# Overflow buffers of a mixture-of-experts stage in two sets, and the last pair's rows brought to their tokens by a matrix product

## The reference, cut to what matters

```
def hierarchical_moe(h, w_rg, b_rg, w_re, b_re, w_gate, w_up, w_down):
    ...
    weights = (g_w * e_w).astype(h.dtype)
    expert = (g_idx * EXPERTS_PER_GROUP + e_idx).reshape(-1)
    ...
    hg = lax.ragged_dot(xs, w_gate, sizes)
    hu = lax.ragged_dot(xs, w_up, sizes)
    ys = lax.ragged_dot(jax.nn.silu(hg) * hu, w_down, sizes)
    ys = ys[inv].reshape(N, TOP_K, D)
    out = jnp.einsum('nkd,nk->nd', ys, weights)
```

## Time and profile before

| | us |
|---|---|
| median of three runs | 1244.88 |
| the profiled execution | 1245.46 |
| its span, first to last instruction | 1243.7 |
| PE busy in it | 1151.6 (93%) |
| DVE, ACT, POOL busy | 663.8, 524.6, 102.8 |
| weights and everything else moved | 252.67 MB, mean 203 GB/s |

### The profile page before, as it was taken

How to read it: one execution, slowest core, us unless ns; L and a number is a source line. 1 busy time by engine, 2 the same in 40 slices (tenths; PEclk the granted TensorE clock), 3 DMA queues, 4 the chain that set the end, 5 groups by cost and what they waited for, 6 DMA issues and landing times.

```text
span 1243.7 us, 20589 instructions
## 1 busy us (share of the span) xinstructions
PE 1151.6 (93%) x8444; PEld 972.2 (78%) x8444; DVE 663.8 (53%) x1217; ACT 524.6 (42%) x916; POOL 102.8 (8%) x165
## 2 busy tenths in 40 slices
PE   6999999999999999989999999899987899889893
PEld 4888788999999888888999998878876654545451
DVE  4555567888745455467898745676445411111113
ACT  5444445555533434544665643464532211111112
POOL 5000000000000000000040000000100022111110
PEclk9999989999999999989999999899996999999897
DMA  9444446777455343336876556333263599999962
GB/s 291 139 153 152 144 138 189 215 230 203 155 185 169 119 170 129 125 119 188 233 207 177 180 171 186 102 102 103 69 245 128 203 420 419 416 418 386 361 279 110
DMA packets 199512, 252.67 MB, mean 203 GB/s; under 512 B 19807, under 2 KB 179083, under 8 KB 187131
## 3 DMA queue, kind: packets, MB, share of 16 engines
q1 hardware_dynamic: 185312, 223.55, 52.9%
q0 software_dynamic: 13744, 27.67, 6.4%
q10 hardware_dynamic: 363, 0.14, 0.0%
HBM read 273.34 MB, written 11.53 MB: 229 GB/s over the span
## 4 chain that ended last, share of the span: by engine, by line
PE 75%; DVE 7%; DMA 6%; ACT 5%; issue 3%; POOL 1%; DVEq 0%; ACTq 0%; POOLq 0%; SPq 0%
PE ps L775 17%; PE ps L776 16%; PE ps L777 16%; PE ps L2512 7%; PE ps L2525 3%; DMA wo<-in_w_exp_gate,wrow 3%; DMA wo<-in_w_exp_down,wrow 2%; ACT whi L747 2%; PE ps L717 2%; PE ps L2115 2%; DVE wlo L756 1%; PE ps L2116 1%; PE ps L2182 1%; PE ps L2504 1%; DMA wo<-in_w_exp_up,wrow 1%
## 5 line engine op out<-in xcount | busy, mean ns | idle before, releaser
L775 PE MATMUL ps<-xhi,whi 128*128 128x272 f32 (+2 forms) x1424 | 428.9, 301 | 20.4 <-DVE xlo L771 10.9
L776 PE MATMUL ps<-xlo,whi 128*128 128x272 f32 (+2 forms) x1424 | 412.6, 290 | 0.0
L777 PE MATMUL ps<-xhi,wlo 128*128 128x272 f32 (+2 forms) x1424 | 411.5, 289 | 0.0
L756 DVE TENSOR_TENSOR wlo<-raw,whi 128x2048 fp32r<-128x2048 f32 (+1 forms) x115 | 259.6, 2257 | 158.6 <-ACT whi L747 158.5
L775 PEld LDWEIGHTS ps<-xhi,whi 128*128 128x128 f32 x1424 | 274.3, 193 | 35.0 <-issue 25.2
L747 ACT ACTIVATE whi<-raw 128x2048 fp32r<-128x2048 f32 (+1 forms) x115 | 216.2, 1881 | 149.8 <-PE ps L777 149.7
L776 PEld LDWEIGHTS ps<-xlo,whi 128*128 128x128 f32 x1424 | 274.0, 192 | 0.9 <-issue 0.5
L777 PEld LDWEIGHTS ps<-xhi,wlo 128*128 128x128 f32 x1424 | 273.3, 192 | 0.0
L775 PE MATMUL ps<-hhi,whi 128*128 128x272 f32 (+1 forms) x352 | 100.7, 286 | 0.7 <-DVE wlo L756 0.6
L776 PE MATMUL ps<-hlo,whi 128*128 128x272 f32 (+1 forms) x352 | 100.2, 285 | 0.0
L777 PE MATMUL ps<-hhi,wlo 128*128 128x272 f32 (+1 forms) x352 | 99.9, 284 | 0.0
(11 more groups left out here) (420 smaller groups left out, 1589.6 us busy)
## 6 DMA issues: line engine op xcount, KB each, us to landing
raw<-in_w_up SPq DMA_DIRECT2D x88, 512.0 KB
raw<-in_w_in SPq DMA_DIRECT2D x33, 1024.0 KB
ada<-in_w_ada POOLq DMA_DIRECT2D x48, 512.0 KB, 5.1
raw<-in_w_exp_gate SPq DMA_DIRECT2D x16, 1024.0 KB
raw<-in_w_exp_up SPq DMA_DIRECT2D x16, 1024.0 KB
wx<-in_w_exp_down SPq DMA_DIRECT2D x16, 1024.0 KB
wy<-in_w_exp_gate SPq DMA_DIRECT2D x16, 1024.0 KB
raw<-in_w_down SPq DMA_DIRECT2D x16, 896.0 KB
```

The source lines that it names most:

```text
L756: dve.tensor_tensor(wlo[SLOT[n]][:, 0:nk, :], raw[n % RAW][:, 0:nk, :], whi[SLOT[n]][:, 0:nk, :].bitcast(F32), ALU.subtract).then_inc(s_w_ ...
L775: pe.matmul(dst, ah, bh, start=first, stop=False, **kw)
L776: pe.matmul(dst, ah, bl, start=False, stop=False, **kw)
L777: return pe.matmul(dst, al, bh, start=False, stop=last, **kw)
```

## The change

It has four parts.

1. *Two sets of overflow buffers.* wo2 (over the tiles place, OH and others of the sort) and wo3 (over constants of earlier stages, set to zero by POOL once) join wo0 and wo1. Even phases use the first set, odd ones the second, whose gathers count on a semaphore of their own. The gather of phase f waits for phase f - 2, and is issued one iteration earlier, ahead of the overflow pair's scatter.
2. *The last pair's rows by a product.* Pair 15 isn't scattered any more. POOL scatters zeros to its rows of spread at the start, SP loads all rows when the other scatters are through, and TensorE multiplies the rows in Yb with last_rows, a matrix of slots by tokens that holds the gate where a slot belongs to a token; DVE adds the result (four more additions). last_rows is made in pairs 0 to 2: a comparison, `gates()` moved to pair 1, and a product that spreads the gates over the partitions.
3. *Residual and gain earlier.* Their transposes and products now stand in iteration 15, and ACT and DVE copy them from PSUM to Xtok and gain.
4. *The order of the tail*: both token halves are scaled and added before the squares.

The diff, cut to its core:

```diff
@@ -54,6 +54,8 @@
 HG_BANK = [5, 7]
+RESID_BANK = [(0, 3), (6, 7)]
+LAST_BANK = [(1, 2), (0, 3)]
 SORT_BANK = [0, 1, 2, 3, 4, 5, 7, 6]
@@ -292,13 +297,15 @@
         Xs = sb("Xs", [P, KT, SLOTS + CAP], at=m)
+        rt = sb("rt", [P, 2, 160], at=m)
+        wo_at = m[0]
         P_at = m[0]
         place = sb("place", [P, 2, SLOTS], F32R, at=m)
-        rt = sb("rt", [P, 2, 160], at=m)
         OH, OHv = sb("OH", [P, 2, 2, NEXP], at=m), sb("OHv", [P, 2, 2, NEXP], at=m)
...
         over, nth = sb("over", [P, 3, NEXP], at=m), sb("nth", [P, 3 * NEXP], at=m)
+        assert m[0] - wo_at >= 4 * 8 * CW
         wy = [sb(f"wy{i}", [P, 8, CW], at=m) for i in range(2)]
@@ -338,6 +345,11 @@
         wo.append(over_tile("wo1", (xlo_at, 4 * KT * T), [P, 8 * CW]))
+        last_rows = over_tile("last_rows", (rs_at, 8 * T), [P, SLOTS])
+        Xtok = over_tile("Xtok", (xlo_at, 4 * KT * T), [P, 2, D])
+        gain = over_tile("gain", (ones_at, ones_end - ones_at), [P, D])
+        wo.append(over_tile("wo2", (wo_at, 4 * 8 * CW), [P, 8 * CW]))
+        wo.append(over_tile("wo3", (ones_at, ones_end - ones_at), [P, 8 * CW]))
         xsl = over_tile("xsl", (xhi_at, 4 * KT * T), [P, 2, 2, KT, CAP])
@@ -878,7 +891,7 @@
                 sp.dma_start(ebuf[u], expert_rows(kind)[P * e:P * e + P, :]).then_inc(ebuf_sem[u], 16)
-            sp.wait_ge(s_scat[0], 16 * ((len(Y_ORDER) + 1) // 2))
+            sp.wait_ge(s_scat[0], 16 * (len(Y_ORDER) // 2))
             sp.wait_ge(s_scat[1], 16 * (len(Y_ORDER) // 2))
@@ -990,13 +1003,14 @@
                     pool.wait_ge(s_over.sem, s_over.after())
-                else:
-                    q_, kind_ = PHASES[f - 1]
+                    fill(wo[3][:, :], 0.0)
+                if f >= 2:
+                    q_, kind_ = PHASES[f - 2]
                     pool.wait_ge(s_w_used.sem, s_w_used.after((kind_, 0, OVERS[q_][1]), 0))
                 for half_, e in enumerate(OVERS[q]):
-                    pool.indirect_dma_start(out=wo[half_][:, :], out_offset=None, in_=expert_rows(kind),
+                    pool.indirect_dma_start(out=wo[2 * (f % 2) + half_][:, :], out_offset=None, in_=expert_rows(kind),
                                             in_offset=bass.IndirectOffsetOnAxis(ap=wrow[:, e - NEXP:e - NEXP + 1], axis=0),
-                                            bounds_check=NEXP * P - 1, oob_is_err=False).then_inc(s_small, 16)
+                                            bounds_check=NEXP * P - 1, oob_is_err=False).then_inc(s_small if f % 2 == 0 else s_gather, 16)
 
@@ -1008,17 +1022,22 @@
 
+            pool.wait_ge(s_htk.sem, s_htk.after(1, 1))
+            fill(Yb[:, 1, :], 0.0)
             pool.wait_ge(s_dest.sem, s_dest.after(0))
-            for p in range(NPAIR + 1):
+            pool.indirect_dma_start(out=spread[:, :], out_offset=bass.IndirectOffsetOnAxis(ap=dest[:, NPAIR - 1:NPAIR], axis=0),
+                                    in_=Yb[:, 1, :], in_offset=None, bounds_check=SLOTS - 1,
+                                    oob_is_err=False).then_inc(s_scat[1], 16)
+            for p in range(NPAIR):
                 if p >= 1:
...
                 f, q, kind = phase_at(p)
+                if phase_at(p + 2)[0] is not None:
+                    load_overflow(*phase_at(p + 2))
                 if kind == "dn":
...
                     return_rows(OVERS[q])
-                if phase_at(p + 1)[0] is not None:
-                    load_overflow(*phase_at(p + 1))
 
@@ -1381,8 +1400,8 @@
                 act.wait_ge(s_w_used.sem, s_w_used.after(("dn", 0, ab[1]), 0))
-                if y >= 2:
-                    act.wait_ge(s_scat[y % 2], 16 * (y // 2))
+                if y:
+                    act.wait_ge(s_scat[y % 2], 16 * (y // 2 + y % 2))
                 act.activation(Yb[:, y % 2, 0:512], ps[4 + 2 * (y % 2)][:, :], ACT.Copy).then_inc(s_y_left.sem, s_y_left.event(y))
@@ -1417,12 +1436,19 @@
                     take_over_a(phase_at(p + 1)[1])
+                if p == NPAIR - 1:
+                    for t in range(2):
+                        act.wait_ge(s_resid.sem, s_resid.after(t, 0))
+                        act.activation(Xtok[:, t, 0:512], ps[RESID_BANK[t][0]][:, :], ACT.Copy).then_inc(s_tail_act.sem, s_tail_act.event("resid", t))
+                    act.wait_ge(s_gain.sem, s_gain.after(0))
+                    act.activation(gain[:, 0:512], ps[0][:, :], ACT.Copy).then_inc(s_tail_act.sem, s_tail_act.event("gain"))
             act.preload_act_table_set("natural_log_exp_and_others")
...
                 act.activation(yl[:, t, 0, :], yl[:, t, 0, :], ACT.Copy, scale=rt[:, t, 107:108]).then_inc(s_tail_act.sem, s_tail_act.event("tail_a", t))
-                act.wait_ge(s_tail_dve.sem, s_tail_dve.after("tail_y", t))
+            for t in range(2):
+                act.wait_ge(s_tail_dve.sem, s_tail_dve.after("tail_z", t, 1))
                 act.activation(yl[:, t, 0, :], yl[:, t, 1, :], ACT.Square, accum_out=ss[:, t:t + 1]).then_inc(s_tail_act.sem, s_tail_act.event("tail_sq", t))
@@ -2057,25 +2083,41 @@
                     row_of(0, ps[7][0:CAP, 0:NEXP:2], ps[7][CAP:P, 1:NEXP:2], slice(0, NEXP // 2))
+                    r(dve.tensor_scalar(last_rows[:, :], iota[:, :], 1.0, inv[:, NPAIR - 1:NPAIR], ALU.add, ALU.is_equal))
                     overflow()
+                if p == 1:
+                    gates()
+                if p == 2:
+                    dve.wait_ge(s_moe_sums.sem, s_moe_sums.after("gates"))
+                    r(dve.tensor_tensor(last_rows[:, :], last_rows[:, :], ps[3][:, :], ALU.mult))
+                    dve.tensor_tensor(last_rows[:, 0:T2], last_rows[:, 0:T2], last_rows[:, T2:2 * T2], ALU.add).then_inc(s_tail_dve.sem, s_tail_dve.event("last_rows"))
+                if p == NPAIR - 1:
+                    for t in range(2):
+                        dve.wait_ge(s_resid.sem, s_resid.after(t, 1))
+                        dve.tensor_copy(Xtok[:, t, 512:1024], ps[RESID_BANK[t][1]][:, :]).then_inc(s_tail_dve.sem, s_tail_dve.event("resid", t))
+                    dve.wait_ge(s_gain.sem, s_gain.after(1))
+                    dve.tensor_copy(gain[:, 512:1024], ps[3][:, :]).then_inc(s_tail_dve.sem, s_tail_dve.event("gain"))
                 if phase_at(p + 1)[2] == "ga":
                     take_over_b(phase_at(p + 1)[1])
-            gates()
             for t in range(2):
...
             for t in range(2):
+                dve.wait_ge(s_tail_dve.sem, s_tail_dve.after("tail_y", t))
+                for h in range(2):
+                    dve.wait_ge(s_resid.sem, s_resid.after("last", t, h))
+                    cs = slice(512 * h, 512 * h + 512)
+                    dve.tensor_tensor(yl[:, t, 1, cs], ps[LAST_BANK[t][h]][:, :], yl[:, t, 1, cs], ALU.add).then_inc(s_tail_dve.sem, s_tail_dve.event("tail_z", t, h))
+            dve.wait_ge(s_tail_act.sem, s_tail_act.after("gain"))
+            for t in range(2):
                 dve.wait_ge(s_tail_act.sem, s_tail_act.after("tail_rt", t))
                 for h in range(2):
-                    if t == 0:
-                        dve.wait_ge(s_gain.sem, s_gain.after(h))
                     cs = slice(512 * h, 512 * h + 512)
-                    dve.scalar_tensor_tensor(yl[:, t, 1, cs], yl[:, t, 1, cs], ss[:, t:t + 1], ps[4 + h][:, :], ALU.mult, ALU.mult).then_inc(s_tail_dve.sem, s_tail_dve.event("tail_n", t, h))
+                    dve.scalar_tensor_tensor(yl[:, t, 1, cs], yl[:, t, 1, cs], ss[:, t:t + 1], gain[:, cs], ALU.mult, ALU.mult).then_inc(s_tail_dve.sem, s_tail_dve.event("tail_n", t, h))
                 for h in range(2):
                     dve.wait_ge(s_tail_dve.sem, s_tail_dve.after("tail_n", t, h))
-                    dve.wait_ge(s_resid.sem, s_resid.after(t, h))
                     cs = slice(512 * h, 512 * h + 512)
-                    dve.tensor_tensor(yl[:, t, 1, cs], ps[2 * t + h][:, :], yl[:, t, 1, cs], ALU.add).then_inc(s_tail_dve.sem, s_tail_dve.event("done", t, h))
+                    dve.tensor_tensor(yl[:, t, 1, cs], Xtok[:, t, cs], yl[:, t, 1, cs], ALU.add).then_inc(s_tail_dve.sem, s_tail_dve.event("done", t, h))
 
@@ -2577,13 +2619,18 @@
 
+                if f == 0:
+                    pe.wait_ge(s_tail_dve.sem, s_tail_dve.after("last_rows"))
                 if kind == "ga":
...
                         pe.wait_ge(s_hut_copied.sem, s_hut_copied.after("over", q - 1))
-                pe.wait_ge(s_small, SMALL_ALL + 32 * (f + 1))
-                weights = [w[:, :] for w in wo]
+                if f % 2 == 0:
+                    pe.wait_ge(s_small, SMALL_ALL + 32 * (f // 2 + 1))
+                else:
+                    pe.wait_ge(s_gather, 32 * (f // 2 + 1))
+                weights = [w[:, :] for w in wo[2 * (f % 2):2 * (f % 2) + 2]]
                 if kind == "dn":
@@ -2617,22 +2664,42 @@
                     narrow(p - 1)
+                if p == NPAIR - 1:
+                    y_banks_free(Y_ORDER.index(PAIRS[p]))
+                    for t in range(2):
```

(37 more changed lines are left out.)

8 lines of the change are left out of this document (6 added, 2 removed).

## The result

The changed kernel takes 1236.42 us (median of 7 executions, 1233.32 to 1239.06) against 1247.43 (7, 1243.68 to 1251.42): ratio 0.991, 95% interval 0.9891 to 0.9929. That is 11.0 us less, where 20.1 was forecast. A second measurement gave 0.9904 (0.9875 to 0.9934). So the change gains about one per cent; the forecast of 1225.4 and its whole range up to 1236 were too low. (Of the experiments' executions three took 1308, 1310 and 3776 us; the ratios leave them out.) The profiled execution took 1236.63 us with a span of 1234.9, as much as the median.

What follows compares the result with a forecast made beforehand. The prediction took TensorE's stalls on late overflow gathers, then the weight loads at 418 GB/s, as the bound. Its terms -17.7 + 4.5 - 6.9 = -20.1 us gave 1225.4 us from 1245.5, range 1218 to 1236.

Steps and rivals of the forecast that it cites:

- The bound: Expert stretch: TensorE loses 28.0 us to late empty gathers; weight loads at 418 GB/s allow 10.2 us back from holes.
- 1.5 us of early work under cover: Expert stretch: added gate products and one DVE operation in early pairs, 1.5 us together, cost nothing under the loads' cover.
- Term 1: Two sets of wo: the last pair's first product moves from 1203.5 to 1185.8, set by the loads, -17.7 us.
- The 10.0 us: End of the loads: the last pair's gate weights land two loads of 2.1 MB, 10.0 us, before the last load.
- Terms 2 and 3: Products moved into the last pair, all on the path, +4.5 us; the tail after the last copies, -6.9 us.
- The scatter of pair 14: Tail: issued at about 1194.5, lands 2.63 (quiet queue) to 10.95 us later; the low end was taken.
- Rival 1: Expert stretch: holes in the loads stay as buffers are released late; 1230.5 with half back, 1235.6 with none; chance 0.14.
- Rival 4: Expert stretch: waits for weights bunch and halve TensorE's clock, 2.6 us in each of 12 pairs; 1248 us; chance 0.04.
- The range: Whole kernel: 1218 to 1236 us, reaching down nearly to full-pace TensorE and up to the end of holes staying.

Runs made afterwards that it cites:

- e5_again: The changed kernel unchanged, for a second profile and more executions; 256.4 us from the experts' first product to the end.
- e1: The kernel before with the two sets of overflow buffers alone, last pair and tail as before; 1234.0 us, ratio 0.9896.
- e6_tail: The changed kernel with residual transposes and gain products moved off the last pair's path and an earlier ACT table load; 1227.99 us, ratio 0.9868.
- e4_spread: The changed kernel with each expert's slots laid over the partitions in steps of four, same bytes; 1235.02 us, ratio 0.9898.
- e11_no_gathers: The changed kernel without 20 of its 24 gathers of overflow weights; 1233.04 us.
- e8_packed: The changed kernel with the first 16 slots laid on two groups of DMA engines in place of four, same bytes; 1242.3 us, ratio 0.9971.

## Why the prediction was wrong

- **The bound, and what each part does: right.** No wait for wo, 1 us a pair for weights, the holes filled, the loads the next limit. The forecast's 1.5 us of early work under cover is there (1.8 us more from the first turn to the third, 24.2 in e5_again against 22.4 in e1) and costs nothing: s to L is 218.8 and 218.9.
- **Term 1, the step that failed:** "So the last load, with the window's end at 1206, would land at 1195.8", and "its gate weights are there only two loads of 2.1 MB (10.0 us) before the last lands: 1195.8 - 10.0 = 1185.8". Bytes over the queue's rate give when the average engine is done. Counted from the stretch's start the forecast has the last load at 224.1 us; in e6_tail and e1 the mean of the 16 engines is at 224.7 and 224.5, and the last of them at 228.6 and 228.8. The 10.0 us held (9.9). So the last pair's first product comes 218.8 us after the start where the forecast had 214.1: 4.7 us. Term 1 measured, from s to L: -12 to -13 instead of -17.7. The kernel before couldn't show it at its end, since the holes had just been there; it showed it in its middle, as a spread growing to 6.3 us, which the forecast didn't use. What pulls the engines apart is for the most part the uneven rows (9.7 to 3.1 without them); what the last 3.1 us are from stays open.
- **The start, not a step of the sum but taken as given by it:** the sum was made against one execution with an early start (971.7). By the medians, before is 2 us and the changed kernel up to 5 us later than the best. In the changed kernel's first profile this is 4.8 us of later start and 1.5 to 2 more for a first product at half clock. 4.8 + 2.0 + 4.7 are the 11.5 us that L was late. So of the 9.1 us that the gain fell short by the medians (11.0 instead of 20.1), about half is the mis-sized term; the rest is in the starts.
- **Terms 2 and 3: right.** +4.5 (16.8 to 21.3), as forecast; -7.1 (23.4 to 16.3) against -6.9. The scatter of pair 14 took the quiet 2.6 us and the loaded rows were not waited for.
- **The rivals.** Rival 1's time (1230.5 to 1235.6) was nearest, but not its mechanism: no hole stayed. Rival 4 is out for the changed kernel: the granted clock was full from 979.6 us to the tail, with waits of up to 1.7 us. It isn't out as such: waits of 2.06 us (e4_spread), 2.37 (e11_no_gathers), 2.05 and 1.95 (e8_packed) were each followed by 3.4 us at half clock, while one of 2.2 in e5_again was not.
- **The range** had only losses by holes above the forecast, 1236 at most. The spread between engines and the start's scatter were no cases of it, and with them 1238 was as near as 1228.

## What to carry to other kernels

Where loads bound a stretch, don't take bytes over rate: look at the first and the last of a load's landing events, whether the gap grows, and which small transfers share the queue with which partitions; and expect that gap to grow further once a change fills the holes in which it closed. Split an execution at a mark that the change doesn't touch and that stands where the bound begins (here the first load), and compare the pieces: the totals here scatter by 6 to 11 us with the clock ahead of the mark, the pieces from s by 2, those from f by 0.4, and the tail by less than 0.2. A product that is put into the last iteration is on the path unless it fills a wait that is already there.

## What was new of the hardware

- DMA engines under one saturated queue drift apart: 9.8 us between first and last after 220 us, at a mean rate of 417 GB/s that shows none of it. The sign in the windows is the end: 0.82 share and 341 GB/s from 1187 to 1206 us, with the first engines out of work.
- Where a scattered row lies matters: 0.11 to 0.15 us a pair for each row of 4 KB on the fullest engine, with the rows divided among engines as assumed above.
- A copy through permuted slots can take longer for the same elements: 1.09 us instead of 0.63 on ACT and 0.62 instead of 0.43 on DVE in e4_spread, 0.69 and 0.43 in e8_packed. Only the first pair's copies were on the path: TensorE waited 3.06 us instead of 2.61 ahead of s.
